# Two layers and a mixer, five norms: the last slabs of a product run tile by tile, with the norm's first turns among them

## What is computed

```
for l in range(2):
    h = rms_norm(x, attn_pre_g[l]);  proj = h @ w_in[l]
    mixed = attention heads of proj (4 differential, 8 forgetting)
    x = x + rms_norm(mixed @ w_out[l], attn_post_g[l])
    h = rms_norm(x, ffn_pre_g[l])
    y = (silu(h @ w_gate[l]) * (h @ w_up[l])) @ w_down[l]
    x = x + rms_norm(y, ffn_post_g[l])
h = rms_norm(x, g_norm_mix);  x = x + merged(mlstm(h), nsa(h)) @ w_out_2
h = rms_norm(x, g_norm_ffn);  x = x + (silu(h @ w_gate_2) * (h @ w_up_2)) @ w_down_2
out = rms_norm(x, g_final)
```

## Time and profile before

| | us |
|---|---|
| median of 3 runs (lowest, highest) | 2246.1 (2245.96, 2246.89) |
| profiled execution, its own time | 2241.13 |
| its span, first to last instruction | 2239.8 |
| PE busy | 2119.8 (95%) |
| DVE, ACT, POOL busy | 988.2, 814.8, 227.0 |
| mean granted clock of PE | 0.987 |

### The profile page before, as it was taken

One profiled execution on the slowest core, in us unless ns is written; L12 is line 12 of the kernel. 1 busy time (PEld: TensorE's weight loads), 2 busy tenths in 40 slices (PEclk: granted clock), 3 DMA queues, 4 the chain that ended last, 5 costly groups with the idle time before them and its releaser, 6 DMA issues. The chain is left out here.

```text
span 2239.8 us, 25576 instructions
## 1 busy us (share of the span) xinstructions
PE 2119.8 (95%) x10364; PEld 1703.8 (76%) x10364; DVE 988.2 (44%) x1833; ACT 814.8 (36%) x1574; POOL 227.0 (10%) x256
## 2 busy tenths in 40 slices
PE   6899899999998999999999998999798999999997
PEld 5667688888887767688888887878655788888886
DVE  6265453323336375453323336645456444323333
ACT  4145442222234255452222225344256334222322
POOL 3003410000000004310000000000156101000000
PEclk9999999999999999999999999999999999999999
DMA  6521123333322311223233332322411233333321
GB/s 155 110 76 57 57 73 109 97 97 97 103 86 69 108 43 63 67 84 102 92 99 97 96 98 58 98 57 81 104 43 38 67 111 92 94 97 101 94 92 68
DMA packets 273721, 192.10 MB, mean 86 GB/s; under 512 B 22060, under 2 KB 241364, under 8 KB 273604
## 3 DMA queue, kind: packets, MB, share of 16 engines
q1 hardware_dynamic: 268704, 177.76, 27.2%
q0 software_dynamic: 4752, 12.67, 2.4%
q10 hardware_dynamic: 148, 0.04, 0.0%
HBM read 186.21 MB, written 4.23 MB: 85 GB/s over the span
## 5 line engine op out<-in xcount | busy, mean ns | idle before, releaser
L593 PE MATMUL bank<-h_features,weights_hi_lo 128*128 128x512 f32 (+1 forms) x5160 | 1131.4, 380 | 9.5 <-POOL h_features L1915 7.8
L593 PEld LDWEIGHTS bank<-h_features,weights_hi_lo 128*128 128x128 f32 x5160 | 928.7, 189 | 196.0 <-issue 14.8
L927 DVE TENSOR_TENSOR weights_hi_lo<-weights,weights_hi_lo 128x1024 fp32r<-128x1024 f32 (+1 forms) x337 | 402.5, 1198 | 702.2 <-ACT weights_hi_lo L1532 701.7
L1532 ACT ACTIVATE weights_hi_lo<-weights 128x1024 fp32r<-128x1024 f32 (+1 forms) x337 | 341.0, 1016 | 393.1 <-PE bank L635 346.2
L633 PE MATMUL bank<-weights_hi_lo,hidden 128*128 128x512 f32 x528 | 205.4, 389 | 0.0
L634 PE MATMUL bank<-weights_hi_lo,hidden 128*128 128x512 f32 x528 | 205.4, 389 | 0.0
L635 PE MATMUL bank<-weights_hi_lo,hidden 128*128 128x512 f32 x528 | 205.4, 389 | 0.0
L1648 ACT ACTIVATE hidden<-arena 128x512 fp32r<-128x512 f32 x66 | 41.7, 632 | 300.1 <-DVE arena L1078 300.1
L1943 POOL TENSOR_SCALAR arena<-arena,row_stats 128x256 f32<-128x256 f32 (+5 forms) x140 | 126.8, 916 | 170.6 <-DVE row_stats L1004 63.4
L1915 POOL TENSOR_TENSOR h_features<-arena,h_features 128x512 fp32r<-128x512 f32 x24 | 30.7, 1278 | 988.8 <-ACT h_features L1560 988.8
L1078 DVE TENSOR_TENSOR arena<-bank,arena 128x512 f32<-128x512 f32 x66 | 45.6, 692 | 181.3 <-PE bank L593 181.3
(11 more groups left out here) (335 smaller groups left out, 2053.8 us busy)
## 6 DMA issues: line engine op xcount, KB each, us to landing
weights<-in_w_in_dram SPq DMA_DIRECT2D x84, 512.0 KB, 3.9
weights<-in_w_gate_dram SPq DMA_DIRECT2D x66, 512.0 KB, 3.8
weights<-in_w_up_dram SPq DMA_DIRECT2D x66, 512.0 KB, 3.8
weights<-in_w_down_dram SPq DMA_DIRECT2D x60, 512.0 KB, 3.6
weights<-in_w_out_dram SPq DMA_DIRECT2D x24, 512.0 KB, 3.7
bias_rows<-decay_scratch POOLq DMA_DIRECT2D x16, 256.0 KB, 4.0
weights<-in_w_cmp_dram SPq DMA_DIRECT2D x16, 256.0 KB, 4.6
weights<-in_w_down_dram SPq DMA_DIRECT2D x12, 256.0 KB, 2.6
```

What stands on the lines that cost most here:

```text
L593: last = e.matmul(out_ap, l, r, start=(j == 0), stop=(j == len(pairs) - 1))
L927: e.tensor_tensor(pair_view(i, 1), raw_view(i), pair_view(i, 0).bitcast(F32), ALU.subtract).then_inc(done, tick(("split", i)))
L1532: e.activation(pair_view(i, 0), raw_view(i), ACT.Copy).then_inc(done, tick(("hi", i)))
```

## The change

- `TAIL` is 3: in the five token products ahead of a norm the last three slabs run tile by tile (in the very last product, which no norm of this kind follows, the tail stays 2).
- PE turns rows 0 and 1 (`first_turns`) ahead of the last token tile of that group, then row 2, begins two tiles, turns row 3 and begins a third tile.
- DVE makes diagonal t right after row t is added. In row 2's turn it also scales rows 0 and 1, and then splits the slabs of the first and second begun tiles, ahead of row 3. Rows 2 and 3 and the third slab follow.
- ACT takes factor t right after the squares of row t, and splits the first two slabs ahead of row 3.
- In "L0 attn" the four diagonals move behind the small copies, into the new order.
- In the feed-forward and the mixer one further split is moved ahead.

The same edits as for "L0 ffn" are made at the other products; the diff shows the first of them.

```diff
+TAIL = 3
...
-    def token_tiles(name, width, source, kt, ready=None, tail=1):
+    def token_tiles(name, width, source, kt, ready=None, tail=1, ahead=None):
         outs = [None] * NT
         step = SLAB // width
         starts = list(range(0, kt, step))
         for group in [[k0] for k0 in starts[:-tail]] + [starts[-tail:]]:
             slabs = [slab((*name, k0)) for k0 in group]
             for t in range(NT):
+                if ahead is not None and t == NT - 1 and group[-1] == starts[-1]:
+                    ahead()
...
+    def turn(s, t):
+        for k0 in (0, 4):
+            out_ap = bank((s, "turn", t, k0))
+            pe.wait_ge(dve.done, dve[s, "diag", t])
+            for k in range(4):
+                last = e.matmul(out_ap[:, k * P:(k + 1) * P], X[:, t, (k0 + k) * P:(k0 + k + 1) * P], DIAG[:, t, :],
+                                start=True, stop=True)
+            last.then_inc(done, tick((s, "turn", t, k0)))
+    def first_turns(s):
+        for t in range(NT - 2):
+            turn(s, t)
     def turn_norm(s, begin):
-        for t in range(NT):
-            for k0 in (0, 4):
-                out_ap = bank((s, "turn", t, k0))
-                pe.wait_ge(dve.done, dve[s, "diag", t])
-                for k in range(4):
-                    last = e.matmul(out_ap[:, k * P:(k + 1) * P], X[:, t, (k0 + k) * P:(k0 + k + 1) * P], DIAG[:, t, :],
-                                    start=True, stop=True)
-                last.then_inc(done, tick((s, "turn", t, k0)))
+        turn(s, NT - 2)
         pe.wait_ge(dve.done, dve[s, "lo", 1, 0])
         pe.wait_ge(pool.done, pool[s, "lo", 1, 4])
-        for name in begin:
+        for name in begin[:2]:
             begin_tile(name, HT)
+        turn(s, NT - 1)
+        begin_tile(begin[2], HT)
         pe.wait_ge(dve.done, dve[s, "lo", 3, 0])
         pe.wait_ge(pool.done, pool[s, "lo", 3, 4])
...
-    def feed_forward(s):
+    def last_slabs(after, half):
+        if after is None or half == 0:
+            return 1 + half, None
+        return TAIL, lambda: first_turns(after)
+    def feed_forward(s, after=None):
         for c in range(NCHUNK):
             for f in range(NFC * c, NFC * (c + 1)):
                 feature_tile((s, "gate", f * P), HT)
                 feature_tile((s, "up", f * P), HT)
             for half in range(2):
                 token_tiles((s, "down", c, half), 512, HIDDEN, NFC,
-                            lambda k, t: pe.wait_ge(dve.done, dve[s, "hidden", NFC * c + k]), 1 + half)
+                            lambda k, t: pe.wait_ge(dve.done, dve[s, "hidden", NFC * c + k]), *last_slabs(after if c == NCHUNK - 1 else None, half))
...
+    first_turns("L0 attn")
+    turn_norm("L0 attn", [("L0", "forget"), ("L0", "qk", C_QA), ("L0", "qk", C_KA)])
...
-            token_tiles((s, "out", half), 512, MIXED, ND, mixed, 1 + half)
-        turn_norm(f"{s} ffn", [(s, "gate", 0), (s, "up", 0)])
-        feed_forward(s)
+            token_tiles((s, "out", half), 512, MIXED, ND, mixed, *last_slabs(f"{s} ffn", half))
+        turn_norm(f"{s} ffn", [(s, "gate", 0), (s, "up", 0), (s, "gate", P)])
+        feed_forward(s, NORMS[2 * layer + 2])
         if layer < LAYERS - 1:
-            turn_norm(f"L{layer + 1} attn", [(f"L{layer + 1}", "forget"), (f"L{layer + 1}", "qk", C_QA)])
+            turn_norm(f"L{layer + 1} attn", [(f"L{layer + 1}", "forget"), (f"L{layer + 1}", "qk", C_QA), (f"L{layer + 1}", "qk", C_KA)])
...
-    def turned_norm(s, gain, first, late):
+    def scaled_turn(s, gain, t):
+        for k0 in (0, 4):
+            tmp4 = turn_slot((s, t, k0))
+            bank = full((s, "turn", t, k0))
+            e.tensor_tensor(tmp4, bank[:, :].rearrange("p (k n) -> p k n", k=4),
+                            VC[:, gain + k0:gain + k0 + 4].unsqueeze(2).to_broadcast([P, 4, P]), ALU.mult
+                            ).then_inc(done, tick((s, "scaled", t, k0)))
+            banks.leave(dve, (s, "turn", t, k0))
+    def low_turn(s, t):
+        tmp4 = turns[s, t, 0].rearrange("p (k n) -> p k n", k=4)
+        dve.wait_ge(act.done, act[s, "hi", t, 0])
+        e.tensor_tensor(HT[:, 1, 0:4, t * P:(t + 1) * P], tmp4,
+                        HT[:, 0, 0:4, t * P:(t + 1) * P].bitcast(F32), ALU.subtract
+                        ).then_inc(done, tick((s, "lo", t, 0)))
+        turns.leave(dve, (s, t, 0))
+    def turned_norm(s, gain, first, rows):
         for t in range(NT):
-            if late and t == 1:
-                diag(s, NT - 1)
-            for k0 in (0, 4):
-                tmp4 = turn_slot((s, t, k0))
-                bank = full((s, "turn", t, k0))
-                e.tensor_tensor(tmp4, bank[:, :].rearrange("p (k n) -> p k n", k=4),
-                                VC[:, gain + k0:gain + k0 + 4].unsqueeze(2).to_broadcast([P, 4, P]), ALU.mult
-                                ).then_inc(done, tick((s, "scaled", t, k0)))
-                banks.leave(dve, (s, "turn", t, k0))
-            tmp4 = turns[s, t, 0].rearrange("p (k n) -> p k n", k=4)
-            dve.wait_ge(act.done, act[s, "hi", t, 0])
-            e.tensor_tensor(HT[:, 1, 0:4, t * P:(t + 1) * P], tmp4,
-                            HT[:, 0, 0:4, t * P:(t + 1) * P].bitcast(F32), ALU.subtract
-                            ).then_inc(done, tick((s, "lo", t, 0)))
-            turns.leave(dve, (s, t, 0))
-            if t == 1:
+            rows(t)
+            if t == NT - 2:
+                scaled_turn(s, gain, 0)
+                low_turn(s, 0)
+            if t < NT - 1:
+                diag(s, t)
+            if t == NT - 2:
+                scaled_turn(s, gain, 1)
+                low_turn(s, 1)
                 splits(SLAB_AT[first] + 2)
+        scaled_turn(s, gain, 2)
+        diag(s, NT - 1)
+        low_turn(s, 2)
         splits(SLAB_AT[first] + 3)
+        scaled_turn(s, gain, 3)
+        low_turn(s, 3)
...
     def hidden_tiles(s, c):
         for f in range(NFC * c, NFC * (c + 1)):
+            splits(SLAB_AT[s, "gate", 0] + 4)
...
-    for t in range(NT):
-        diag("L0 attn", t)
...
-        for half in range(2):
-            slabs_of((s, "out", half), ND, 512, 1 + half)
-            for t in range(NT):
-                weigh_rows(s, half, t, False)
-                if half == 1:
-                    add_rows(s, t, False)
-                    if t >= 1:
-                        diag(f"{s} ffn", t - 1)
-        turned_norm(f"{s} ffn", VEC["ffn_pre"] + ND * layer, (s, "gate", 0), True)
+        slabs_of((s, "out", 0), ND, 512, 1)
+        for t in range(NT):
+            weigh_rows(s, 0, t, False)
+        slabs_of((s, "out", 1), ND, 512, TAIL)
+        def rows(t):
+            weigh_rows(s, 1, t, False)
+            add_rows(s, t, False)
+        turned_norm(f"{s} ffn", VEC["ffn_pre"] + ND * layer, (s, "gate", 0), rows)
...
-        if m > 0:
-            splits_for(("M", "mqk", C_MQ + m * P))
+        splits_for(("M", "mqk", C_MQ + m * P))
...
+    turned_norm("ffn2", VEC["ffn2_pre"], ("M", "gate", 0), lambda t: add_to_x(("M", "out", 1), t, 1))
...
-    def turned_norm(s, first):
+    def high_turn(s, t):
+        for k0 in (0, 4):
+            act.wait_ge(dve.done, dve[s, "scaled", t, k0])
+            e.activation(HT[:, 0, k0:k0 + 4, t * P:(t + 1) * P], turns[s, t, k0].rearrange("p (k n) -> p k n", k=4),
+                         ACT.Copy).then_inc(done, tick((s, "hi", t, k0)))
+    def turned_norm(s, first, rows):
         for t in range(NT):
-            for k0 in (0, 4):
-                act.wait_ge(dve.done, dve[s, "scaled", t, k0])
-                e.activation(HT[:, 0, k0:k0 + 4, t * P:(t + 1) * P], turns[s, t, k0].rearrange("p (k n) -> p k n", k=4),
-                             ACT.Copy).then_inc(done, tick((s, "hi", t, k0)))
-            if t == 1:
+            if t == NT - 1:
                 splits(SLAB_AT[first] + 2)
+            rows(t)
+            if t >= NT - 2:
+                high_turn(s, 2 * (t - NT + 2))
+            if t == NT - 2:
+                high_turn(s, 1)
         splits(SLAB_AT[first] + 3)
+        high_turn(s, 3)
```

More of the change, by code:

```diff
@@ L1878, in scalar_program, with rows @@
                 tables()
[L1879 to L1881 removed]
+                slabs_of(("M", "out", 0), ND, 512, 1)
+                slabs_of(("M", "out", 1), ND, 512, TAIL)
+                def rows(t):
                     act.wait_ge(dve.done, dve[("M", "out", 1), "x", t])
                     row_norm("ffn2", t)
[L1884 removed]
+                turned_norm("ffn2", ("M", "gate", 0), rows)
                 hidden_tiles("M", 0)
```

88 lines of the change are left out of this document (38 added, 50 removed).

## The result

| | before | changed kernel |
|---|---|---|
| median us (lowest, highest) | 2246.0 (2245.5, 2246.9) | 2270.8 (2261.0, 2276.3) |
| ratio, 95% interval | | 1.0108 [1.0083, 1.0132] |
| profiled execution, us; its span | 2241.13; 2239.8 | 2260.97; 2259.7 |
| TensorE: busy, sum of its waits, us | 2119.8, 107.8 | 2128.3, 118.7 |

A forecast was written before the change was run, and what follows sets the result against it. TensorE, busy 95%, was taken as the bound, leaving only its waits to win. The norms, mixer and layer 0 summed to +17 us: 2258 for the profiled execution, 2263 for the median, range 2249 to 2278.

The forecast's parts named there:

- the rival of the falling clock: TensorE's clock falls behind new waits of up to 2.7 us; one fall in each of five norms +12, 2275; chance 0.15.
- the group's waits: TensorE waits for the third slab's split before a group: 2.6 us at three out products, 1.6 at two down.
- diagonal 1: In L1 attn, TensorE waits 2.7 us for row 1's diagonal, which comes at 14.7 us from the group's start.
- the begun tile: In L1 attn, the first begun tile waits 2.4 us for its split, which stands behind row 1's low part.
- a row's round in L1 attn: DVE waits for ACT's factor before the next row: about 5.5 us a row, against a tile's 3.4 on TensorE.
- Diagonal 2: Starting with POOL's low part, it takes 1.30 us instead of 0.29: 1.2 more per norm, 6 in the sum.
- L0 ffn and L1 ffn 2 x (2.3 + 0.5): Two feed-forward norms: idle 6.4 us where 4.1 were, plus 0.5 each for the third begun tile; 5.6 in sum.
- L1 attn 2.2 + 0.5: Layer 1's attention norm: idle 11.7 us where 9.5 were, plus 0.5 for the third begun tile; 2.7 in sum.
- the last waits of 0.7 and 1.4: In L1 attn, turn 3 waits 0.7 us and the third begun tile 1.4 for its split.
- layer 0: L0 attn norm: later turns and 2 MB write add 3.6 to 6.1 us; 4.5 taken, one more slab landing first.
- The mixer: The 1.2 us wait for the third convolution tile's split goes; 0 to 2 come back later, 1 taken.
- The first rival: Rows keep pace with tiles: 28.7 us of idle go, 11 and 2.7 come; -15, so 2231; chance 0.05.

The follow-up runs named there:

- e5: Changed kernel with TensorE's old turn order and first norm as before, three slabs, waits at each slab's first use, rows added early on VectorE: 2239.9 us, ratio 0.9984.
- e1: Changed kernel with one edit: TensorE waits for each slab's split right ahead of its first matmul, not for all three ahead of the group: 2247.8 us, ratio 1.0016.
- e3: Changed kernel with the first norm (L0 attn) as before the change: 2263.2 us, ratio 1.0078.
- e6: e4 with the first norm as before the change: 2237.0 us, ratio 0.9965.
- e4: Changed kernel with e1's edit, rows staggered on VectorE and ScalarE as before, and two begun tiles' splits one place earlier: 2242.2 us, ratio 0.9987.
- e7: Changed kernel with its new TensorE waits filled by matmuls on the identity whose results are overwritten: 2261.0 us, ratio 1.0083.

## Why the prediction was right, and where not

The measured 2270.8 lies within the stated range of 2249 to 2278, but above the 2259 to 2268 of the forecast with its bounds. It is within the range because that took in the rival of the falling clock, and this rival came true beside the forecast's own case.

**Right by its own steps:** slower, by new waits at the places named: the group's waits, 2.56 and 1.60 (2.6 and 1.6 expected, modelled end apart); diagonal 1, 2.53 (2.7); the begun tile, 2.33 (2.4); a row's round in L1 attn: VectorE starts adding at 688.43, 693.90 and 699.37, 5.47 us apart (5.5). Diagonal 2 took 1.30 us, as expected:

```profile
705.77 1.30 DVE L962 TENSOR_SCALAR diag_rstd<-shape_consts,norm_stats 128x128 f32<-128x128 f32 x1
```

In each of the five norms it took 1.30 to 1.34, against 0.29 for the others, so 1.0 us more; the 1.2 a norm, and the 6 us in all, of the prediction are a little more than its rows give, and no run was made without it. The Trainium skill (SBUF — State Buffer, Who interferes with whom) calls the port pair an exclusive lock. The traces agree, also for two low parts and for a low part beside a split (e5).

**Mis-sized, upward:** the terms "L0 ffn and L1 ffn 2 x (2.3 + 0.5)" and "L1 attn 2.2 + 0.5". Per norm 1.0 to 2.1 us at full clock against 2.7 and 2.8. In L1 attn diagonal 2's wait was 2.12 for 2.7, and the last waits of 0.7 and 1.4 did not come as such: turn 3 had none, the third tile 0.41. TensorE was at half clock just then and reached them later; a wait and a slow stretch that overlap are paid once. In e1, where the begun tiles ran at full clock, the two stand at 0.53 and 1.10.

**Mis-sized, downward:** the term "layer 0". 4.5 was taken between 3.6 and 6.1; it was 6.4 from trace to trace, and 4.2 (e3) and 5.5 (e6 against e4) at full clock over several executions. The sentence "because one more slab lands ahead of the write" failed: the two waits end 35.6 to 35.8 and 47.6 to 47.9 us behind the write's issue in the three traces above, and the issue moved from 40.59 to 46.90. So the waits took up the whole delay of the write, 6.3 us, and not a part of it.

**The mixer:** the wait of 1.22 went, and one of 1.89 came at the value product (at 1447.79), within the 0 to 2 that were to come back.

**The clock:** here the forecast was right on the time and wrong on the case. It gave the falls 0.15, arguing that waits of up to 2.7 us lie between 1.55, which had slowed nothing, and 3.91. The mixer of the same trace spoke against that: there a fall stands right behind a wait of 1.61 us, and one more at 1654.9 behind 1.55, while waits of up to 1.79 in L1 attn had none, so that length alone did not decide it (TensorE, then a stretch as above; kernel before):

```profile
1528.62 0.47 PE L830 MATMUL bank<-shape_consts,arena 128*128 128x128 f32 x1 [1.61 <-DVE arena L1365]
...
1530.00:1532.00 2.00, 2.00 (x7) 1.63 (x6) 0.80 (x4) 0.74 (x3) 0.00 (x0) 0.50 0.00 0
```

The rival's 12 us came, though not by its sum: seven falls of 1.7 us, where five of 2.4 were reckoned. That the profiled execution's +19.9 comes near +17 is in part luck: 5 of it are falls, and it had 7 us less of them in the mixer than before. 13 of the median's 25 us are the rival's. The sum at full clock was 12 to 15 for 17, so without the falls the median would have been some 2258 to 2261. e7 shows the cause: waits filled, no falls in the norms.

**The first rival's sum** leaves out layer 0's 4.5 us, which it says stays; with it the rows that keep pace would have given about 2236, not 2231. No chance hangs on that.

## What to carry to other kernels

When a wait for several buffers stands ahead of a group, wait at each buffer's first use: four lines took back 23 of 25 us here. Before giving an engine more to do in a tight stretch, lay the steps of VectorE and GpSimd side by side as well as in order, since two low parts at once cost more than either; the best order here came from that. And price a new wait on TensorE twice, once by its length and once by the clock behind it, taking several executions, as one profile may show the lucky case: the first one here had the norms' 12 us of falls, and hid 7 of them by fewer falls in the mixer.
